# Key factors spread from turned rows, first convolution taps on ScalarE, and output weights split three attention steps later

## The reference

```python
h    = rms_norm(x, norm1_g) * (1 + scale1) + shift1
proj = h @ w_in                       # 1472 columns: c_q 256, c_kv 128, k_rope 64, conv_u 1024
q = rms_norm(rms_norm(c_q) @ w_uq)    # 4 heads x 192, the norm is over each head
k = rms_norm([rms_norm(c_kv) @ w_ukv (nope part), k_rope])   # the same k_rope in each head
o = softmax(rope(q) rope(k)^T / sqrt(192)) @ v
a, g = conv_u halves;  y = a * sigmoid(g)
y = conv(y, 31 taps, one filter per channel, 512 channels) + conv_b
conv_out = silu(layer_norm(y))
x = x + gate1 * (concat(o, conv_out) @ w_out)
x = x + gate2 * experts(rms_norm(x) ...)   # 16 experts, each takes its best 64 tokens
```

## Time and profile before

| | |
|---|---|
| median of 3 runs | 2679.06 us (2676.0 to 2679.06) |
| the profiled execution: time, span | 2672.59 us, 2670.9 us |
| PE busy | 2480.8 us, 93% |
| DVE, ACT, POOL busy | 1123.1, 851.2, 307.4 us |
| granted TensorE clock, mean | 0.963 |
| attention loop, layer 1, first scores to last value product | 170 to 252 us |
| the same, layer 2 | 965 to 1047 us |

### The profile page before, as it was taken

The page is one execution under the profiler, slowest core; times in us unless marked ns, Lnnn a source line. Parts: engine busy times, 40 slices in busy tenths (PEclk is TensorE's granted clock), DMA queues, the critical chain, the costliest instruction groups (busy, mean ns, idle before and its releaser), DMA issues. The chain is left out here.

```text
span 2670.9 us, 31960 instructions
## 1 busy us (share of the span) xinstructions
PE 2480.8 (93%) x12976; PEld 1479.0 (55%) x12976; DVE 1123.1 (42%) x1736; ACT 851.2 (32%) x1161; POOL 307.4 (12%) x122
## 2 busy tenths in 40 slices
PE   5989799999997989799999996999999999989998
PEld 4734533333335735433333334887788787766665
DVE  4985312222224885312222225565322112456765
ACT  4235111111114245111111115566432344245553
POOL 0002000000000011000000002001433452200000
PEclk8999899999998989899999997999999999989999
DMA  9702579999999502489999993322233331149995
GB/s 344 265 1 80 204 303 409 410 410 410 410 408 336 204 0 95 190 337 409 410 410 410 409 394 95 91 83 80 79 103 102 102 120 64 48 166 375 360 352 205
DMA packets 276277, 646.27 MB, mean 242 GB/s; under 512 B 12098, under 2 KB 110656, under 8 KB 276160
## 3 DMA queue, kind: packets, MB, share of 16 engines
q1 hardware_dynamic: 269038, 631.78, 63.0%
q0 software_dynamic: 2592, 7.87, 0.8%
q10 hardware_dynamic: 4528, 4.98, 0.6%
HBM read 639.88 MB, written 6.29 MB: 242 GB/s over the span
## 5 line engine op out<-in xcount | busy, mean ns | idle before, releaser
L759 PE MATMUL ps<-ring,scr 128*64 128x512 f32 x1952 | 428.3, 596 | 1.4 <-DMA ring<-in_w_up 1.4
L759 PEld LDWEIGHTS ps<-ring,scr 128*64 128x64 f32 x1952 | 139.1, 138 | 280.9 <-issue 275.4
L1432 POOL TENSOR_TENSOR raw_r<-raw,w_high 128x2048 fp32r<-128x2048 f32 (+1 forms) x44 | 192.4, 4379 | 464.9 <-ACT w_high L1686 464.9
L781 PE MATMUL ps<-ring,scr 128*64 128x512 f32 x1024 | 230.2, 603 | 1.4 <-ACT scr L953 1.4
L1448 PE MATMUL ps<-x_high,w_high 128*128 128x512 f32 x480 | 195.0, 406 | 10.7 <-DVE y L2067 5.7
L1450 PE MATMUL ps<-x_high,raw_r 128*128 128x512 f32 x480 | 191.2, 398 | 0.0
L1449 PE MATMUL ps<-xT_r,w_high 128*128 128x512 f32 x480 | 190.5, 397 | 0.0
L1009 DVE SCALAR_TENSOR_TENSOR one_hot_T<-h_tok,convw,one_hot_T 128x512 f32<-128x512 f32 x240 | 170.4, 763 | 1.7
L469 POOL TENSOR_TENSOR one_hot_T_r<-hy,one_hot_T_r 128x1024 fp32r<-128x1024 f32 x16 | 38.5, 2409 | 1121.5 <-ACT one_hot_T_r L965 1121.5
L1218 DVE TENSOR_TENSOR scr<-scr,ps 128x512 f32<-128x512 f32 x32 | 22.0, 688 | 318.7 <-PE ps L759 318.7
L2558 DVE TENSOR_TENSOR ring_r<-ring,ring_high 128x2048 fp32r<-128x2048 f32 x56 | 127.7, 2288 | 63.5 <-ACT ring_high L2436 63.4
(11 more groups left out here) (528 smaller groups left out, 4398.8 us busy)
## 6 DMA issues: line engine op xcount, KB each, us to landing
ring<-in_w_down SPq DMA_DIRECT2D x64, 2048.0 KB, 15.2
ring<-in_w_up SPq DMA_DIRECT2D x62, 2048.0 KB, 18.3
ring<-in_w_gate SPq DMA_DIRECT2D x60, 2048.0 KB, 14.9
ring<-in_w_up SPq DMA_DIRECT2D x56, 1024.0 KB, 7.6
ring<-in_w_ada SPq DMA_DIRECT2D x22, 2048.0 KB, 12.5
ring<-in_w_down SPq DMA_DIRECT2D x28, 1024.0 KB, 7.2
raw<-in_w_in SPq DMA_DIRECT2D x23, 1024.0 KB, 5.1
ring<-in_w_in SPq DMA_DIRECT2D x16, 512.0 KB, 10.4
```

Of the source, the lines that this page charges most:

```text
L759: mm = pe.matmul(ps[CAP * half:CAP * (half + 1), 1 + j // 2, :], x_e[:, at_x:at_x + CAP], weights[:, k, half * HALF:(half + 1) * HALF], st ...
L781: mm = pe.matmul(ps[CAP * half:CAP * (half + 1), 4, :], hidT[:, at_f:at_f + CAP], weights[:, k, half * HALF:(half + 1) * HALF], start=(j = ...
L1432: pool.tensor_tensor(dst, src, high.bitcast(F32), ALU.subtract).then_inc(w_ready, 1)
```

## The change

Three edits, in both layers.

1. The key factors: PE turns `rqk` once (128x32 to 32x128), DVE copies it out into `key_rows`, and for each head PE makes four products of 128 columns each, whose stationary matrix is one column of the identity repeated: this picks one row and puts it on all partitions. `key_diag` is gone. The product for the router's bias moves from bank 7 to bank 5.
2. The first tap of each channel group goes to ACT (one `activation` with scale and bias), queued in ACT's program of tiles 1, 3, 5 and 11 between `ada_kept` and `w_in_split_tile`. DVE makes 30 taps for each group. The tables of taps change with it.
3. The rounding of `w_out` moves from steps 3 to 10 to steps 6 to 13, and POOL's subtractions follow it.

```diff
-ALONE = 14
-TAPS_IN_TILE = (0, 5, 9, 9, 10, 10, 10, 10, 6, 4, 2, 4)
+ALONE = 13
+TAPS_IN_TILE = (0, 5, 8, 9, 10, 10, 10, 10, 7, 4, 0, 6)
 TAPS_IN_HEADS = 24
-TAPS_IN_STEP = (4, 4, 4, 3, 3, 3)
+TAPS_IN_STEP = (2, 3, 3, 3, 3, 3)
...
-    left, out = [list(range(TAPS)) for _ in range(CT)], []
+    left, out = [list(range(1, TAPS)) for _ in range(CT)], []
...
# PE
             pe.wait_ge(head_root, 1)
             for t in range(TT):
                 mm = pe.transpose(ps[:, 7, t * P:(t + 1) * P], head_rms[:, t * P:(t + 1) * P], ident)
             mm.then_inc(head_cols, 1)
-            def key_factor(h):
-                pe.wait_ge(kd_ready, h + 1)
-                if h >= 1:
-                    pe.wait_ge(qk_ready, h)
-                pe.matmul(ps[:, 6, :], ones[:], kd, start=True, stop=True).then_inc(kb_mm, 1)
+            def key_factor(h):
+                if h >= 1:
+                    pe.wait_ge(qk_ready, h)
+                for t in range(TT):
+                    row = 2 * (HEADS * t + h) + 1
+                    mm = pe.matmul(ps[:, 6, t * P:(t + 1) * P], ident[0:GROUP, row:row + 1].to_broadcast([GROUP, P]), key_rows, start=True, stop=True)
+                mm.then_inc(kb_mm, 1)
+            pe.wait_ge(rqk_ready, 1)
+            pe.transpose(ps[0:GROUP, 7, 0:P], rqk, ident).then_inc(rqk_turned, 1)
+            pe.wait_ge(key_rows_kept, 1)
             key_factor(0)
...
# ACT, input tiles
                 if at_tile < 8:
                     ada_kept(4 + at_tile, 6)
+                if i < 2 * CT and i % 2 == 1:
+                    c = i // 2
+                    act.wait_ge(vec_ready, 2)
+                    act.wait_ge(dve_proj, c + 1)
+                    act.activation(acc[:, c, :], ypad[:, c, 0:S], ACT.Identity, bias=vec[:, CB + c:CB + c + 1], scale=convw[:, c:c + 1]).then_inc(conv_first, 1)
...
# ACT, attention steps
-                if 3 <= i < 3 + KT:
-                    kt = i - 3
+                if 6 <= i < 6 + KT:
+                    kt = i - 6
...
# DVE
-                    if t == 0:
-                        dve.wait_ge(dve_proj, c + 1)
-                        op = dve.tensor_scalar(acc[:, c, :], src, w, vec[:, CB + c:CB + c + 1], ALU.mult, ALU.add)
+                    if t == 1:
+                        dve.wait_ge(conv_first, c + 1)
...
+            dve.wait_ge(rqk_turned, 1)
+            dve.tensor_copy(key_rows, ps[0:GROUP, 7, 0:P]).then_inc(key_rows_kept, 1)
-            key_diag(0)
             key_norm(0)
...
-                    if i // TT + 1 < HEADS:
-                        if i % TT == 0:
-                            key_diag(i // TT + 1)
-                        if i % TT == 2:
-                            key_norm(i // TT + 1)
+                    if i // TT + 1 < HEADS and i % TT == 2:
+                        key_norm(i // TT + 1)
```

More of the change, by code:

```diff
@@ L330, in layer @@
     mx, nmx, rsum, rrs, rqs, rqk = (stat[:, a:b] for a, b in ((0, 16), (16, 32), (32, 48), (48, 64), (64, 80), (80, 112)))
-    root, head_rms, kd = M["krg"][:, 0:P], rin[:, 2, :], rin[:, 3, :]
+    root, head_rms, key_rows = M["krg"][:, 0:P], rin[:, 2, :], rin[0:GROUP, 3, 0:P]
     root2 = scr[:, 3, 0:2 * P]
@@ L355, in layer @@
     lat_sq, lat_ss, lat_root, lat_inv, lat_bc, lat_ready = (sem(n) for n in ("lat_sq", "lat_ss", "lat_root", "lat_inv", "lat_bc", "lat_ready"))
-    qk_mm, qk_ev, rot_mm, roped, head_ss, head_root, head_cols, kd_ready, kb_mm, qk_ready = (
-        sem(n) for n in ("qk_mm", "qk_ev", "rot_mm", "roped", "head_ss", "head_root", "head_cols", "kd_ready", "kb_mm", "qk_ready"))
+    qk_mm, qk_ev, rot_mm, roped, head_ss, head_root, head_cols, rqk_ready, rqk_turned, key_rows_kept, kb_mm, qk_ready = (
+        sem(n) for n in ("qk_mm", "qk_ev", "rot_mm", "roped", "head_ss", "head_root", "head_cols", "rqk_ready", "rqk_turned", "key_rows_kept", "kb_mm", "qk_ready"))
     s_done, nm_ready, exp_done, prob_ready, t_done, pt_ev, pv_done, pv_ev = (
         sem(n) for n in ("s_done", "nm_ready", "exp_done", "prob_ready", "t_done", "pt_ev", "pv_done", "pv_ev"))
-    conv_tap, cmean, cdev, csq, cvar, croot, cinv, cbc, cnorm, cmix = (
-        sem(n) for n in ("conv_tap", "cmean", "cdev", "csq", "cvar", "croot", "cinv", "cbc", "cnorm", "cmix"))
+    conv_first, conv_tap, cmean, cdev, csq, cvar, croot, cinv, cbc, cnorm, cmix = (
+        sem(n) for n in ("conv_first", "conv_tap", "cmean", "cdev", "csq", "cvar", "croot", "cinv", "cbc", "cnorm", "cmix"))
     wout_done, x1_ready = sem("wout_done"), sem("x1_ready")
@@ L627, in _ @@
             pe.wait_ge(pad_zero, 1)
+            pe.wait_ge(qk_ev, 14)
             for kt in range(KT):
-                mm = pe.matmul(ps[:, 7, 0:GROUP], mod[:, SHIFT2 + kt:SHIFT2 + kt + 1].to_broadcast([P, P]), w_r[:, kt, :], start=(kt == 0), stop=(kt == KT - 1))
+                mm = pe.matmul(ps[:, 5, 0:GROUP], mod[:, SHIFT2 + kt:SHIFT2 + kt + 1].to_broadcast([P, P]), w_r[:, kt, :], start=(kt == 0), stop=(kt == KT - 1))
             mm.then_inc(r_bias_mm, 1)
-            pe.wait_ge(qk_ev, 14)
             pe.wait_ge(roped, 3)
@@ L655, in _ @@
                     pe.wait_ge(pt_ev, TT * (h + 1))
+                    if h == 0:
+                        pe.wait_ge(r_bias_kept, 1)
                     if h >= 1:
@@ L661, in _ @@
                 if i == 7:
-                    pe.wait_ge(r_bias_kept, 1)
-                    pe.wait_ge(conv_tap, CT * TAPS)
+                    pe.wait_ge(conv_tap, CT * (TAPS - 1))
                     for c in range(CT):
@@ L1003, in convolve @@
                     w, src = convw[:, t * CT + c:t * CT + c + 1], ypad[:, c, t:t + S]
-                    if t == 0:
-                        dve.wait_ge(dve_proj, c + 1)
-                        op = dve.tensor_scalar(acc[:, c, :], src, w, vec[:, CB + c:CB + c + 1], ALU.mult, ALU.add)
+                    if t == 1:
+                        dve.wait_ge(conv_first, c + 1)
                     else:
                         dve.wait_ge(conv_tap, last[c])
-                        op = dve.scalar_tensor_tensor(acc[:, c, :], src, w, acc[:, c, :], ALU.mult, ALU.add)
-                    op.then_inc(conv_tap, 1)
+                    dve.scalar_tensor_tensor(acc[:, c, :], src, w, acc[:, c, :], ALU.mult, ALU.add).then_inc(conv_tap, 1)
                     last[c] = n + 1
@@ L1073, in _ @@
             dve.wait_ge(head_cols, 1)
-            step(dve.reciprocal(rqk, ps[:, 7, :].rearrange("p (n k) -> p n k", k=GROUP // 2)[:, :, 0]))
-            step.settle()
+            dve.reciprocal(rqk, ps[:, 7, :].rearrange("p (n k) -> p n k", k=GROUP // 2)[:, :, 0]).then_inc(rqk_ready, 1)
+            dve.wait_ge(rqk_ready, 1)
             factors = rqk.rearrange("p (t h k) -> p t h k", t=TT, h=HEADS)
             step(dve.tensor_scalar(rqs.rearrange("p (h t) -> p t h", h=HEADS), factors[:, :, :, 0], QSCALE, None, ALU.mult))
-            def key_diag(h):
-                dve.tensor_tensor(kd.rearrange("p (t n) -> p t n", t=TT), ident.unsqueeze(1).to_broadcast([P, TT, P]),
-                                  factors[:, :, h, 1].unsqueeze(2).to_broadcast([P, TT, P]), ALU.mult).then_inc(kd_ready, 1)
+            dve.wait_ge(rqk_turned, 1)
+            dve.tensor_copy(key_rows, ps[0:GROUP, 7, 0:P]).then_inc(key_rows_kept, 1)
             def key_norm(h):
@@ L1123, in _ @@
                     dve.wait_ge(r_bias_mm, 1)
-                    dve.tensor_copy(rbias[:], ps[:, 7, 0:EXPERTS]).then_inc(r_bias_kept, 1)
+                    dve.tensor_copy(rbias[:], ps[:, 5, 0:EXPERTS]).then_inc(r_bias_kept, 1)
                 if i == 10:
```

## The result

The changed kernel is slower: median 2693.29 us (2693.06 to 2696.67, 5 runs) against 2679.06 us, ratio 1.0062 with a 95% interval of 1.0047 to 1.0077. The forecast was 2679, with 2687 as its upper end. The profiled execution has a span of 2691.5 us against 2670.9. Of these 20.6 us some 6 are chance: the kernel before, run many times beside the experiments, gave 2669.88 to 2684.84, and its profiled execution was one of the quick ones.

What follows compares the result with a forecast made beforehand. DVE was taken to set PE's pace before the expert weight stream. Per layer 5.05 + 2.5 + 0 - 9.2 + 1.6 = -0.05 us, twice 0, so 2679 us; range 2670 to 2687.

Steps and rivals of the forecast that it cites:

- edit 2 ahead of tile 11: Input tiles: first taps on ACT make DVE's reciprocal of tile 10 come 4.25 us later per layer.
- DVE's two waits of 1.91: Tiles 3 and 5: DVE's subtraction waits for ACT's tap and rounding, +1.91 us each, 3.82 for both.
- PE's pause of 6.2: Ahead of tile 10's spread: PE's idle time grows from 2.43 to about 6.2 us.
- The clock's price there: Behind tile 10's pause: PE at 1.2 GHz costs +2.5 us a layer, at least 1.6, at most 4.4.
- the later rotation of 0.8: Behind tile 11: more DVE taps, +1.7 us, mostly covered by 0.92 idle, leave +0.8.
- It comes out even, 0: First head: turned key rows take as long as the old diagonal and product, 0 within 0.4 us.
- -9.2 for the loop: Attention loop up to step 7: step 7's scores start at 195.9 instead of 205.13, -9.2 us a layer.
- the lower clock as a rival: Steps 2 to 6: PE at 1.2 GHz bounds the loop, 4.4 us a layer lost, 2688; chance 0.22.
- the small waits of the steps: Steps 2 to 6: PE waits of 0.2 to 1.2 us, which must stay under what lowers the clock.
- Its own sign of being wrong: The forecast is wrong, and the kernel slower, if the clock falls in steps 2 to 6.
- +1.6 was forecast for the part behind step 7: From step 8 on: a vanished wait, -1.15, and later rounding and POOL subtractions, +2.75, give +1.6 us a layer.
- the reading that DVE instructions with an operand in PSUM pass POOL's: DVE beside POOL: PSUM operands pass, SBUF ones wait; if `mix_rest` passed, the sum would be 1.3 us a layer lower.

Runs made afterwards that it cites:

- e6: The changed kernel with six spare PE products ahead of tile 10's spread and one on either side of the reciprocals' transpose: 2676.72 us, ratio 1.0004 to the kernel before.
- e3: The kernel before with only the rounding of the output weights moved to steps 6 to 13: 2679.17 us, ratio 0.9992.
- e5: The changed kernel with ACT's first tap queued behind the rounding of its tile's weights instead of ahead: 2683.88 us, ratio 1.0023 to the kernel before.
- e4: The changed kernel with one spare PE product at the first head, ahead of the reciprocals' transpose: 2683.29 us, ratio 1.0004 to the kernel before.
- e1: The kernel before with only the turned key rows in place of the diagonals: 2679.57 us, ratio 1.0002.
- e8: The kernel before with turned key rows, ACT's first taps behind the rounding, taps moved to DVE's idle time, no output-weight rounding in steps 11 and 12: 2664.57 us, ratio 0.9947.
- e2: The kernel before with only the first taps on ACT ahead of the rounding and the new tap tables: 2693.53 us, ratio 1.0053.
- e12: The changed kernel with the output weights rounded in steps 3 to 10 as before: 2696.77 us, ratio 1.0070 to the kernel before.
- e7: The kernel before with DVE's last product with the sines made four times instead of once: 2687.52 us, ratio 1.0031.
- e9: e8 with two spare PE products around the transpose of the reciprocals: 2657.89 us, ratio 0.9929 to the kernel before.

## Why the prediction was wrong

**Right: edit 2 ahead of tile 11.** 4.25 was forecast and 4.28 measured, with DVE's two waits of 1.91 (1.89 measured) and PE's pause of 6.2 (5.94). The clock's price there, taken as 2.5 with 1.6 below it, and the later rotation of 0.8 came to 2.4 and 3.2 together. e6 kept full clock there and has 36.50 for the same stretch, against 35.59: 0.9 is the rotation, and 1.5 and 2.2 are the clock. e3 shows that the kernel before loses 1.6 there in some executions too, so part of this line is not the change's. e5 takes the waits away and wins 9 to 10 us.

**Wrong: "It comes out even, 0", for the first head, and with it -9.2 for the loop.** Both sums held only at full clock. The chain itself is what I said: with the clock at 1.00 the first maximum comes 6.22 us behind the reciprocal, before 6.15, and the pace is 26.4, where 34.98 - 9.2 = 25.8 was forecast (e4, layer 2). But at the first head the clock fell in both layers, the chain took 10.6 and 9.9, and the steps gave back only 4.2 and 4.3. That is 7.5 us a layer by e4's two layers, 9.4 and 8.6 against the forecast. The prediction had the lower clock as a rival (0.22, 2688, just outside its own range of 2670 to 2687) with the right sign and mechanism, PE becoming the bound of steps 2 to 6, and looked for its trigger in the wrong place: in the small waits of the steps. Those can bring a fall too, at 1.7 us a layer in e6, where the first head held. Its own sign of being wrong, the clock falling in steps 2 to 6, is what the trace shows, only that the fall began ahead of step 0.

The prediction never asked what the late rotation and the new chain do to PE ahead of the attention. The pause of 1.32 us held full clock in all four layers of the two traces that have it (the kernel before, e3). Edit 1 turns it into 0.52 and 0.37 us, with short products between, and the clock fell in three of four layers (e1, e8). Edit 2's rotation, 0.9 us later, makes it 2.25 us, and it fell in both layers (e2). Together they give 1.45 and 0.37 us, and it fell in all six layers of the changed kernel, e5 and e12. e7 shows that a later DVE alone can do it. Why the clock falls at one pause and not at another isn't shown; e9's layer 2 fell with no pause.

**Mis-sized: edit 3.** +1.6 was forecast for the part behind step 7, +5.2 and +3.3 measured. `mix_rest` waited for POOL as forecast. Its line in the kernel before, POOL's in the changed kernel (its own there, 238.34, stands above), and the value product behind the spread, before and after:

```profile
231.46 0.68 DVE L1097 TENSOR_TENSOR hy_r<-hy,hy_r 128x512 fp32r<-128x512 f32 x1
```

```profile
237.34 2.41 POOL L463 TENSOR_TENSOR ring_r<-ring,one_hot_T_r 128x1024 fp32r<-128x1024 f32 x1 [2.90 <-ACT one_hot_T_r L927]
```

```profile
236.55 3.60 PE L659 MATMUL ps<-ring 128*128 128x512 f32 x8
```

```profile
246.75 4.85 PE L665 MATMUL ps<-ring 128*128 128x512 f32 x8
```

The Trainium skill's shared port pair (SBUF — State Buffer, "SBUF: two separate sides") gives such a wait for a DVE instruction with two SBUF inputs beside a GpSimd one: the trace agrees, 1.96 us instead of 0.68. Up to PE's spread of step 13 the loss is 1.05 us in both layers (26.86 and 26.85 from the maximum of step 7, before 25.81); e3, where the clock held behind the spread, adds 0.4 for the late scaling. Those stalls come near the 1.6 forecast. What I left out again is what a pause does: behind the 2.15 us the clock fell in both layers of the changed kernel, and from the spread to the scores of step 14 it took 3.3 and 1.4 us longer than before. The last 0.8 and 0.9 lie behind those, around the last value product. Of the reading that DVE instructions with an operand in PSUM pass POOL's, rows 3 and 4 show only the other half; the trace of the kernel before has both (two of L1130 in 1.29 us from 211.27, under POOL's 210.60 to 212.96).

The common flaw: I priced the clock once, at the one long pause, and treated all others as free because the trace of the kernel before had full clock behind them.

## What to carry to other kernels

Where a change makes a PE pause longer, or moves it, price it at the clock behind it, not at its length: here 1.4 us more on DVE (e7) cost 8 to 10 in two layers. List the pauses between a stage's last wide products and the next stage's first ones that a change lengthens or adds; full clock there in one old profile is no proof, not even for the old kernel (e3). When an operation goes to a second engine, look at what the second engine's queue holds back behind it: the same tap one place later in ACT's program was worth 9 to 10 us.

## What the runs showed of the hardware

- The clock fell behind pauses of 0.52 and 0.37 us with short products between them (e8, both layers), and in e9's layer 2 with PE shown busy without a pause for 15 us. One and the same instruction stream does it in one layer and not in the other of one execution (e1, e4, e9). Of the first head's pauses, one of 1.32 us held in four layers of four, 2.25 and 2.75 in none of four. What exactly decides is open; no run here separates it.
- Once down in the changed kernel, it stayed at 0.50 from 174.2 to 201.5 while PE was shown busy throughout, from 179.43 on mostly with products of 512 columns. In layer 1 of e1 it stayed for 20 us beside such work. Around 200.58 in the kernel before it was back after 3.4 us.
- Spare products, which add work to PE, made the changed kernel 15.5 us faster by the ratios, one product (e4) as much as all pauses filled (e6); by the medians it is 10 and 16.6.
